# Two transformer blocks in split fp32: one 512-column matmul for the high and low activations

## The reference

```python
# block 1: feed-forward, D_FF = 2816
up = _causal_dwconv(h @ w_up[l], conv_w[l], conv_b[l])
gate, val = jnp.split(up, 2, axis=-1)
x = x + (1.0 + gate2) * ((jax.nn.silu(gate) * val) @ w_down[l])
# blocks 2 and 3: MLP, width 4096
def sq_relu_mlp(h, w_in, w_out):
    return jnp.square(jax.nn.relu(h @ w_in)) @ w_out
# and the output projections of the mixers, each 1024 x 1024
x = x + (1.0 + gate1) * (y @ w_out)      # "out"
h = h + o @ w_o                          # "wo", "gla_out"
```

## Time and profile before

| | |
|---|---|
| Median of 3 runs | 1101.54 us (1100.02 to 1103.86) |
| Span of the profiled execution, first to last instruction | 1091.4 us |
| TensorE busy | 950.5 us (87% of the span) |
| VectorE, ScalarE, GpSimd busy | 631.9, 502.9, 645.5 us |
| Mean granted TensorE clock | 0.941 of full |

### The profile page before, as it was taken

One profiled execution on the slowest core, in us unless ns is written; L12 is line 12 of the kernel. 1 busy time (PEld: TensorE's weight loads), 2 busy tenths in 40 slices (PEclk: granted clock), 3 DMA queues, 4 the chain that ended last, 5 costly groups with the idle time before them and its releaser, 6 DMA issues.

```text
span 1091.4 us, 17804 instructions
## 1 busy us (share of the span) xinstructions
PE 950.5 (87%) x7373; PEld 910.2 (83%) x7373; DVE 631.9 (58%) x944; ACT 502.9 (46%) x713; POOL 645.5 (59%) x145
## 2 busy tenths in 40 slices
PE   4598678789999997959888999999987698999997
PEld 3587567789999997955678999999987698999997
DVE  5889678885464558996547222225576928323233
ACT  2325743364545545426543444336464553444442
POOL 1355351556878786530176878876645366788883
PEclk8698888899999998979999999999989999999999
DMA  9957443945454545240045555655533334566641
GB/s 353 317 160 248 138 155 120 324 136 185 164 193 155 193 160 187 78 126 1 1 154 177 161 192 188 193 174 156 171 100 116 112 124 137 173 191 197 192 152 40
DMA packets 122283, 177.13 MB, mean 162 GB/s; under 512 B 3088, under 2 KB 103996, under 8 KB 122076
## 3 DMA queue, kind: packets, MB, share of 16 engines
q1 hardware_dynamic: 121260, 173.97, 48.4%
q10 hardware_dynamic: 944, 2.03, 0.6%
HBM read 174.68 MB, written 1.05 MB: 161 GB/s over the span
## 4 chain that ended last, share of the span: by engine, by line
PE 53%; DVE 27%; ACT 7%; issue 6%; POOL 4%; DMA 4%; SPq 0%; DVEq 0%; ACTq 0%; POOLq 0%
PE psum L1414 16%; PE psum L1416 15%; PE psum L1415 15%; POOL w_lo L473 4%; DVE arena L1132 4%; DVE ada L919 4%; ACT w_hi L490 3%; DVE work L836 2%; DVE h_lo L828 2%; PE psum L1682 1%; DVE arena L1186 1%; DMA raw<-in_w_out_dram 1%; DMA rows<-in_g_sgu_dram 1%; DVE a_lo L1140 1%; PE psum L1662 1%
## 5 line engine op out<-in xcount | busy, mean ns | idle before, releaser
L473 POOL TENSOR_TENSOR w_lo<-raw,w_hi 128x2048 fp32r<-128x2048 f32 (+1 forms) x139 | 642.6, 4633 | 426.9 <-ACT w_hi L490 425.7
L1414 PE MATMUL psum<-h_hi,w_hi 128*128 128x256 f32 x1384 | 398.1, 288 | 43.9 <-DVE h_lo L828 11.5
L1415 PE MATMUL psum<-h_lo,w_hi 128*128 128x256 f32 x1384 | 392.3, 283 | 0.0
L1416 PE MATMUL psum<-h_hi,w_lo 128*128 128x256 f32 x1384 | 392.2, 283 | 0.0
L490 ACT ACTIVATE w_hi<-raw 128x2048 fp32r<-128x2048 f32 (+1 forms) x139 | 263.5, 1902 | 154.4 <-PE psum L1416 92.0
L1414 PEld LDWEIGHTS psum<-h_hi,w_hi 128*128 128x128 f32 x1384 | 267.4, 193 | 49.9 <-POOL w_lo L473 24.9
L1415 PEld LDWEIGHTS psum<-h_lo,w_hi 128*128 128x128 f32 x1384 | 267.0, 193 | 0.2
L1416 PEld LDWEIGHTS psum<-h_hi,w_lo 128*128 128x128 f32 x1384 | 266.7, 193 | 0.0
L1414 PE MATMUL psum<-a_hi,w_hi 128*128 128x256 f32 x688 | 192.5, 280 | 5.9 <-DVE a_lo L1140 5.9
L1415 PE MATMUL psum<-a_lo,w_hi 128*128 128x256 f32 x688 | 192.0, 279 | 0.0
L1416 PE MATMUL psum<-a_hi,w_lo 128*128 128x256 f32 x688 | 191.9, 279 | 0.0
(11 more groups left out here) (262 smaller groups left out, 1067.9 us busy)
## 6 DMA issues: line engine op xcount, KB each, us to landing
raw<-in_mlp_w_in_dram SPq DMA_DIRECT2D x32, 1024.0 KB, 5.5
raw<-in_mlp_w_out_dram SPq DMA_DIRECT2D x32, 1024.0 KB, 4.9
raw<-in_w_ada_dram SPq DMA_DIRECT2D x24, 1024.0 KB, 7.5
raw<-in_w_up_dram SPq DMA_DIRECT2D x22, 1024.0 KB, 5.1
raw<-in_gla_w_in_dram SPq DMA_DIRECT2D x12, 1024.0 KB, 5.3
raw<-in_w_down_dram SPq DMA_DIRECT2D x11, 1024.0 KB, 5.1
raw<-in_w_in_dram SPq DMA_DIRECT2D x10, 1024.0 KB, 7.9
raw<-in_attn_w_qkv_dram SPq DMA_DIRECT2D x6, 1024.0 KB, 4.9
```

Source lines behind the costliest of these rows:

```text
L473: pool.tensor_tensor(halved(w_lo, n % SPLIT_SLOTS, key), halved(raw, r % RAW_SLOTS, key), halved(w_hi, n % SPLIT_SLOTS, key).bitcast(F32), ...
L1414: pe.matmul(dst, lhs[0], rhs[0], start=start, stop=False, skip_group_check=True)
L1415: pe.matmul(dst, lhs[0], rhs[1], start=False, stop=False, skip_group_check=True)
L1416: return pe.matmul(dst, lhs[1], rhs[0], start=False, stop=stop, skip_group_check=True)
```

## The change

For the six kinds of chunk in `WIDE` the high and low activations lie side by side in SBUF (`h_both`), and `two` issues one matmul of 512 columns with the high weights, then one of 256 columns with the low weights into the first half. The bank then holds two partial sums: high x high plus low x high in columns 0 to 255, high x low in columns 256 to 511. They are joined where the bank is read. For the output projections DVE adds both halves to the residual, one after the other. For gate, val and mlp_in, ACT copies the second half to SBUF (`second_half`), and DVE adds it to the first half in place (`merge`); all that read the bank before now wait for `merged`. The chunks in, qkv, gla, down and mlp_out keep the three matmuls.

```diff
+WIDE = ("out", "gate", "val", "wo", "gla_out", "mlp_in")
...
+        h_both = sb("h_both", [P, KT, 2, S], F32R)
+        h_hi, h_lo = h_both[:, :, 0, :], h_both[:, :, 1, :]
...
+        part = rows[:, 0:4, :].rearrange("p n c -> p (n c)").rearrange("p (b s) -> p b s", b=2)
+        merges = [(kind, i, f) for i in range(FF_STEPS) for kind in ("gate", "val") for f in range(2)]
+        merges += [("mlp_in", layer, i, f) for layer in range(2) for i in range(MLP_STEPS) for f in range(2)]
...
+            def second_half(*job):
+                n = merges.index(job)
+                act.wait_ge(*at("job", *job))
+                act.wait_ge(*(at("merged", *merges[n - 2]) if n >= 2 else at("job", "rows", len(ROWS) - 1)))
+                act.activation(part[:, n % 2, :], bank(*job)[:, S:2 * S], ACT.Copy).then_inc(*mark("half", *job))
...
             def ff_up(i):
                 ahead(("gate", i))
                 for f in range(2):
-                    act.wait_ge(*at("job", "gate", i, f))
+                    second_half("gate", i, f)
+                for f in range(2):
+                    act.wait_ge(*at("merged", "gate", i, f))
...
                 ahead(("val", i))
                 for f in range(2):
-                    act.wait_ge(*at("job", "val", i, f))
+                    second_half("val", i, f)
+                for f in range(2):
+                    act.wait_ge(*at("merged", "val", i, f))
...
             def mlp_act(layer, i):
+                for f in range(2):
+                    second_half("mlp_in", layer, i, f)
                 for f in range(2):
                     act.wait_ge(*at("dve_read", "mlp_in", layer, i, f))
...
+                    for half in range(2):
+                        src = bank(kind, n, m)[:, half * S:(half + 1) * S]
+                        if half:
+                            dve.wait_ge(*at("half_added", kind, n, m))
...
+            def merge(*job):
+                n = merges.index(job)
+                dve.wait_ge(*at("half", *job))
+                dst = bank(*job)[:, 0:S]
+                dve.tensor_tensor(dst, dst, part[:, n % 2, :], ALU.add).then_inc(*mark("merged", *job))
...
                 for kind, buf, first in (("gate", ff_g, 0), ("val", ff_v, 22)):
+                    for f in range(2):
+                        merge(kind, i, f)
...
                 for f in range(2):
-                    dve.wait_ge(*at("job", "mlp_in", layer, i, f))
+                    merge("mlp_in", layer, i, f)
+                for f in range(2):
+                    dve.wait_ge(*at("merged", "mlp_in", layer, i, f))
...
+            def two(dst, lhs, high, both, start, stop):
+
+
+                pe.matmul(dst[:, 0:2 * S], lhs[0], both, start=start, stop=False, skip_group_check=True)
+                return pe.matmul(dst[:, 0:S], lhs[1], high, start=False, stop=stop, skip_group_check=True)
```

39 lines of the change are left out of this document (20 added, 19 removed).

## The result

The changed kernel is slower: median 1109.93 us (1107.88 to 1110.26, 5 runs) against 1100.79 us (1098.93 to 1103.86, 5 runs) of the kernel before beside it. The ratio is 1.0084, 95% interval 1.0057 to 1.011. The profiled execution has a span of 1106.7 us, of which TensorE is busy 87%, as before.

A forecast was written before the change was run, and what follows sets the result against it. TensorE was taken to bound the MLPs, wo and gla_out, GpSimd's loop the feed-forward. +2.8 - 0.6 - 4.1 - 0.6 - 2.2 = -4.7 us gave a median of 1096.8, range 1090 to 1106 for 8 in 10.

The forecast's parts named there:

- I take 217 for the wide one and the old spacing for the narrow one: 217 + 118 = 335 against 354.: Wide chunks on TensorE: ns per pair against three matmuls at the slow spacing, saving 19 ns, 0.31 us per chunk.
- The MLPs in the steady run: 26 wide mlp_in chunks: TensorE stays the bound, gaining 4.1 us in block 2 and 2.2 in block 3.
- The fit in GpSimd's gap: MLP steady run: four DVE instructions with both inputs in SBUF still fit GpSimd's gap, 0.5 us to spare (0.2 fast spacing).
- the rival of a missed gap: MLPs: DVE misses GpSimd's gap and TensorE waits 3 us each time; 1107 to 1140 us, chance 0.13.
- The feed-forward, +2.8: Gate and val: GpSimd's loop keeps its 17.86 us; gate 1's merges behind DVE's MEMSET cost about 2.8 us once.
- The wait before val: Feed-forward steady loop: the 0.62 us TensorE saves per step become idle time before val, 0.6 becoming 1.2.
- "wo" and "gla_out", -0.6 each: Output projections bound by TensorE end 1.25 us earlier, less 0.4 for the second addition; counted as -0.6 each.
- "out", 0: Output projection waiting for modulation weights and `w_lo`, which do not move: no change.
- This knot moves as a whole: MLP start: DVE instructions stuck behind GpSimd and TensorE's 2.56 us wait for `a_lo` shift together with the first `w_hi`.
- The wide matmul is no cheaper: Rival on wide matmuls: no saving, only +2.8 and two late additions remain; 1104 to 1105 us, chance 0.12.
- The last stretch restarts at 118 ns: Rival in block 3's MLP: slow spacing follows a stall, +1.8 instead of -2.2 us; 1100.8, chance 0.22.
- The offset: Whole kernel: the same 4.7 us taken off the span, 1091.4 to 1086.7, and off the median, 1101.5 to 1096.8.

The follow-up runs named there:

- before_again: The kernel before, unchanged, run and profiled a second time: median 1100.99 us, ratio 1.0014.
- split512: The changed kernel with each 512-column matmul issued as two of 256 columns, joins kept: 1103.78 us, ratio 1.0052 to the kernel before.
- ff_only: The kernel before with wide matmuls and joins in gate and val alone: 1107.27 us, ratio 1.0065.
- late_before: The kernel before with the MEMSET and two small DVE operations moved from feed-forward step 1 to step 3, small ones first: 1095.8 us, ratio 0.9966; repeated 0.996.

## Why the prediction was wrong

Foretold were 4.7 us less, 1096.8 us; measured were 1109.93, 9.1 us more than the kernel before beside it.

- **"I take 217 for the wide one and the old spacing for the narrow one: 217 + 118 = 335 against 354."** This step failed. A pair takes 353 ns, as long as three matmuls at the slow spacing. The 217 came from fp32 records, 2.5 ns above their stream; fp32r matmuls pay 13.3 by themselves, and in the pairs of this kernel the wide one 17 to 24 (230 to 237 less 213) and the narrow one 10 to 17. The second half of the argument, that a wide matmul covers a load that is just exposed at 256 columns, falls too: 256, 320 and 512 columns by themselves all lie 13.3 ns above their stream, so there was no exposed load to save.
- **The MLPs in the steady run, -4.1 and -2.2:** measured +0.05 and +0.04 against 148.68 and 146.99 (before_again). The fit in GpSimd's gap was right: no wait of TensorE, and the rival of a missed gap did not come.
- **The feed-forward, +2.8:** the mechanism was right step by step. Taken from gate 0 (2.30 us later in this profile), GpSimd's operation stands at 249.55 (foretold 249.45), the next at 258.17 (258.1), val 3 at 280.72 (280.6). Gate 0 to qkv 0 went from 205.08 to 207.71, +2.6. Over all profiles with the MEMSET group where it was it is 207.7 to 208.6 with joins (four) and 204.4 to 206.7 without (four), and how long the clock stays at 0.50 behind mod 5 moves it within each group, for which the prediction had no term. Like held against like, the joins cost 2.6 us where that is 3.4 us (after, before) and 1.5 to 2.0 us where it is 6.8 us. The wait before val stays 0.6 and not 1.2, since TensorE saved nothing.
- **"wo" and "gla_out", -0.6 each:** wo +0.43, the second addition with nothing to set against it. gla_out can't be told from its scatter.
- **"out", 0:** open. Gate 0 starts at 217.7 (split512) to 223.6 us with the joins in "out", and at 218.3 to 224.1 without.
- **"This knot moves as a whole":** it did, and it cost time all the same, since the prediction left out the clock. In block 2 the second mlp_out chunk starts 30.8 to 31.0 us after mlp_in 0 in the six profiles with joins there, and 30.5 to 31.1 in nine of the ten without. But TensorE waits 3.1 us before it instead of 1.6 to 2.7 in eight of those nine, and the granted clock then falls to 0.50 in the chunk, which takes 7.25 us instead of 5.73. It fell in all six with joins and in one of the ten without (ff_only, after 3.6 us of waiting). The first steps take 43.7 to 43.9 us against 41.0 to 43.4, 1.5 us between the means. In block 3 it is less sure: the clock fell in five of six with joins and in four of ten without, 40.9 to 43.8 us against 41.0 to 43.5, 0.9 us between the means. Over both blocks, 19 of the 32 waits at this place were 3.1 to 3.6 us long, and the clock fell behind 15 of them; where the wait was shorter or missing (13 times) it fell once, after 2.4 us. So a wait does not settle it alone.
- **The rivals.** "The wide matmul is no cheaper" (0.12, 1104 to 1105) was what happened; its 1104 to 1105 has the feed-forward and the two late additions, and what it lacks is the clock at the start of the MLPs and the part that is not accounted for below. "The last stretch restarts at 118 ns" also happened in the profile, but is no effect of the change.
- **The offset.** The span of 1091.4 was subtracted from the median of other executions. The difference of 10.1 us was not what lies around the span (1.8) but that the profiled execution was quick.

Added up from the profiles: feed-forward 1.5 to 2.6, wo 0.4, MLP starts 1.5 and 0.9, steady run 0.1, together 4.4 to 5.5 of the 7 to 9 us measured. The remaining 2 to 4 us are not accounted for. The stretch ahead of gate 0 scatters by 4 us, enough to hold them, but the runs don't show that it does.

By medians: 0.996 (group moved, no joins), 1.000 (joins in the steady run), 1.0055 (joins everywhere), 1.0069 and 1.0084 (group back in step 1). The version that beats both kernels is late_before, 0.3 to 0.4% under the kernel before.

## What to carry to other kernels

Price an instruction from a row of its own data type: two types that stream alike differed by 11 ns per matmul in bursts (215.8 and 226.7) and by 13 to 20 ns in the kernel, where the expected gain was 10 to 19 ns a triple. Look at the granted clock behind every wait that a change lengthens, also where nothing starts later: it cost 1.5 us at the start of an MLP. Before moving a DVE instruction with both inputs in SBUF, look where GpSimd's operations will stand when it is issued, however small it is: the same 128 x 8 one took 0.15, 1.92 or 3.91 us by its place alone. And take a second profile of the kernel before, since one execution can be 8 us off the median, and any difference to it then reads as an effect.

## What the runs showed of the hardware

- fp32r matmuls: 111.7, 120.0, 146.7, 173.3, 226.7 ns for 128, 256, 320, 384, 512 columns at the full granted clock; 256 and 512 also with the other engines busy, 256 also with unchanged weights. bf16 of 256 columns takes 109.2, a record of fp32 of 256 columns 215.8, one of 128 columns 111.7.
- In this kernel the same 256-column triples come at 117.8 or 113.3 ns, and never at 120.0 for long. What picks the value is open: data, addresses, banks, events, waits and load of the other engines were tried in the bursts and changed nothing.
- Wide and narrow in turn take 353.3 or 346.7 ns a pair in bursts, 353 or (rarely) 349 in the kernels. Three narrow ones take 340, 353 or 360.
- A DVE instruction of 128 x 1024 with two inputs in SBUF (L919) takes 1.28 us, and 3.7 to 5.8 where a GpSimd operation came first. One more of them held ahead of gate 0 goes with 3.5 to 4.3 us.
- At mod 5 TensorE waited 2.2 to 6.7 us in eight profiles, and in each the granted clock was 0.50 there or just behind, for 3.4 to 10.2 us. After a wait of 1.06 us, and in the seven profiles without one, it stayed 1.00.
